# The opening weight loads and the last projection stores of a transformer block: blocks interleaved, 32 matmul passes made 16 transposes, a drain moved into the next stage

## The reference: what is computed

```python
mx = (silu(c) @ w_ada + b_ada)           # 6 x 1024 modulations; mz likewise from c_ctx
u  = x * (1 + mx[1]) + mx[0]             # modulated stream; context by mz
h  = u @ w_in                            # 1024 -> 1824 columns (context: 544 of them)
# A: latent attention, 6 heads (rank 256 for q, 128 for kv, shared rotary key)
# B: grouped attention, 6 query heads on 2 kv heads, RMS-normalised, 2-D rotary
# C: gated convolution of width 3
x  = layer_norm(ALPHA * x + mx[2] * (concat(A, B, C) @ w_o))
x  = layer_norm(ALPHA * x + mx[5] * (relu(x * (1 + mx[4]) + mx[3]) @ w1) ** 2 @ w2)
```

## Time and profile before

| | us |
|---|---|
| three runs: median (lowest to highest) | 3210.21 (3207.03 to 3212.64) |
| the profiled execution, its own time | 3208.03 |
| its span | 3206.2 |
| PE busy in the span | 3057.0 (95%) |
| DVE busy | 2299.8 (72%) |
| 16 DMA engines, queue q1 | 45.9% of their span |

### The profile page before, as it was taken

How to read it: one execution, slowest core, us unless ns; L and a number is a source line. 1 busy time by engine, 2 the same in 40 slices (tenths; PEclk the granted TensorE clock), 3 DMA queues, 4 the chain that set the end, 5 groups by cost and what they waited for, 6 DMA issues and landing times. The chain is left out here.

```text
span 3206.2 us, 38685 instructions
## 1 busy us (share of the span) xinstructions
PE 3057.0 (95%) x13729; PEld 2270.5 (71%) x13729; DVE 2299.8 (72%) x3190; ACT 1343.1 (42%) x1915; POOL 1368.1 (43%) x817
## 2 busy tenths in 40 slices
PE   4999968999999999999999997999999999999997
PEld 2888855565565656656566876888788888888786
DVE  3354446777777777777767788877777767788778
ACT  2232322434444444443443445555555543533441
POOL 0233301576776767755653225333333224323420
PEclk6999978999999999999999998999999999999999
DMA  6222378124332323221214678444733388887784
GB/s 238 61 78 86 97 228 287 56 61 103 89 76 68 73 62 89 61 66 37 49 40 163 241 279 311 159 157 157 290 145 148 141 316 291 302 310 292 271 307 144
DMA packets 235418, 515.49 MB, mean 161 GB/s; under 512 B 26673, under 2 KB 101809, under 8 KB 223025
## 3 DMA queue, kind: packets, MB, share of 16 engines
q1 hardware_dynamic: 227856, 484.97, 45.9%
q10 hardware_dynamic: 7392, 28.31, 2.4%
HBM read 352.44 MB, written 160.76 MB: 160 GB/s over the span
## 5 line engine op out<-in xcount | busy, mean ns | idle before, releaser
L1138 DVE TENSOR_REDUCE h_mpart<-a_mx 128x1 f32<-128x512 f32 x920 | 568.7, 636 | 266.1 <-PE a_mx L1238 257.4
L1075 POOL TENSOR_TENSOR a_acc_p<-a_acc_p,a_pf 128x1024 f32<-128x1024 f32 x240 | 581.0, 2421 | 213.4 <-ACT a_pf L1118 188.0
L1118 ACT ACTIVATE a_pf<-o_y 128x1024 f32<-128x1024 f32 x432 | 442.3, 1024 | 483.1 <-PE o_y L1264 482.6
L2273 PE MATMUL f_bank<-slots,f_wx 128*128 128x512 f32 x2304 | 573.4, 391 | 6.9 <-DMA slots<-s_uc 6.9
L2281 PE MATMUL f_bank<-slots 128*128 128x512 f32 x2128 | 505.4, 390 | 4.7 <-DVE slots L2052 2.5
L2273 PEld LDWEIGHTS f_bank<-slots,f_wx 128*128 128x128 f32 x2304 | 434.6, 189 | 99.1 <-DMA slots<-s_uc 8.5
L2281 PEld LDWEIGHTS f_bank<-slots 128*128 128x128 f32 x2128 | 399.4, 188 | 90.5 <-DVE slots L2052 4.2
L2219 POOL TENSOR_TENSOR f_work<-raw_rows 128x512 f32<-128x512 f32 x160 | 220.4, 1379 | 378.5 <-DVE f_wx L2045 366.6
L2228 POOL TENSOR_TENSOR f_y<-f_y,raw_rows 128x1024 f32<-128x1024 f32 x72 | 195.8, 2719 | 346.1 <-DMA raw_rows<-in_w 346.1
L2066 DVE TENSOR_TENSOR f_work<-f_work,f_bank 128x512 f32<-128x512 f32 x256 | 174.4, 681 | 133.7 <-ACT f_work L1944 122.5
L523 PE MATMUL p_main<-win_hi,u_hi 128*128 128x512 f32 (+2 forms) x528 | 198.2, 375 | 27.6 <-PEq L75 22.6
(11 more groups left out here) (277 smaller groups left out, 5354.7 us busy)
## 6 DMA issues: line engine op xcount, KB each, us to landing
raw_rows<-s_hx SPq DMA_DIRECT2D x112, 512.0 KB, 4.3
f_y<-in_w SPq DMA_DIRECT2D x104, 512.0 KB, 5.4
raw_rows<-in_w SPq DMA_DIRECT2D x72, 512.0 KB, 5.9
raw_rows<-in_w SPq DMA_DIRECT2D x32, 1024.0 KB, 4.8
s_hx<-stream SPq DMA_DIRECT2D x128, 256.0 KB, 2.7
s_hx<-f_work SPq DMA_DIRECT2D x96, 256.0 KB, 2.0
a_wa<-in_w_ada SPq DMA_DIRECT2D x8, 2048.0 KB, 9.3
slots<-s_uc ACTq DMA_DIRECT2D x10, 1024.0 KB, 15.2
```

The lines of the kernel that those rows point to most:

```text
L1075: nc.gpsimd.tensor_tensor(acc[:, :], left[:, :], pf[(b * KT + kt) % NPF][:, :], ALU.add).then_inc(added_p, 1)
L1118: nc.scalar.activation(pf[n % NPF][:, :], sc[n % 2][:, :], ACT.Exp, scale=SCALES[0 if is_mla(b) else 1]).then_inc(exped, 1)
L1138: nc.vector.reduce_max(mpart[b % 2][:, s, k:k + 1], mx[c % 2][:, 0:CHUNKS[k][1]], AX.X).then_inc(mx_read, 1)
L2273: mm = nc.tensor.matmul(by_pair(bank[:, m % 8, :]), w[:, k], x[s][:, :, k * P:(k + 1) * P], start=(k == 0 and j == 0), stop=(k == 3 and j ...
```

## The change

In the first stage SP issues `w_in` blocks 0, 1 and 2 each behind a `w_ada` block (2, 3 and 4), and blocks 3 to 7 behind the context tile. ACT and DVE split blocks 0 to 2 before their part in the modulations, and the rest behind it. The row is turned by 16 `transpose` instructions, each over 2 partitions at the start of a strip, into four PSUM banks, and the bias is added in four parts. The last projection tile's 13 stores no longer stand in the projection: SP issues the seven key/value ones and the two of the convolution at the start of the expansion, ACT the four of the queries behind its first three items. Their semaphore is waited for by SP ahead of `load_ckv` part 2 and by ACT ahead of `load_first_heads`.

```diff
@@ stage_modulate
-        SLOTS, ROWS = 3, 4
+        SLOTS, ROWS, BETWEEN = 3, 4, 3
-        ps = ctx.enter_context(nc.psum_tensor("ada_ps", [P, 512], F32))
+        ps = ctx.enter_context(nc.psum_tensor("ada_ps", [P, 4, 512], F32))
@@ SP
             for k in range(KD):
                 need(sp, w_used, k - SLOTS + 1)
                 sp.dma_start(w[:, k % SLOTS, :], a["w_ada"][k * P:(k + 1) * P, 0:NM]).then_inc(w_in[k % SLOTS], 16)
+                if 2 <= k < 2 + BETWEEN:
+                    w_in_rows(k - 2)
             tile(0)
-            for k in range(KD):
+            for k in range(BETWEEN, KD):
                 w_in_rows(k)
@@ ACT
-            act.wait_ge(w_used, KD)
-            nc.scalar.activation(row_sb[:, :], row_ps[:, :], ACT.Copy).then_inc(turn_step, 1)
             for k in range(KD):
+                if k == BETWEEN:
+                    act.wait_ge(w_used, KD)
+                    nc.scalar.activation(row_sb[:, :], row_ps[:, :], ACT.Copy).then_inc(turn_step, 1)
                 act.wait_ge(rows_in[k % ROWS], 16 * (k // ROWS + 1))
                 nc.scalar.activation(g.w_hi[:, k], rows[k % ROWS], ACT.Copy).then_inc(w_hi_set, 1)
-                if k == 0:
+                if k == BETWEEN:
                     act.wait_ge(g.modulated, 1)
@@ DVE
+            for k in range(BETWEEN):
+                low(k)
...
-            nc.vector.tensor_tensor(g.mods[:, 0:16, :], ps[:, 0:32].rearrange("p (m c) -> p m c", c=2),
-                                    g.b_ada[:, 0:16, None].to_broadcast([P, 16, 2]), ALU.add).then_inc(turn_step, 1)
+            for c in range(4):
+                m = slice(4 * c, 4 * c + 4)
+                ins = nc.vector.tensor_tensor(g.mods[:, m, :], ps[:, c, 0:8].rearrange("p (m c) -> p m c", c=2),
+                                              g.b_ada[:, m, None].to_broadcast([P, 4, 2]), ALU.add)
+            ins.then_inc(turn_step, 1)
...
-            for k in range(KD):
+            for k in range(BETWEEN, KD):
                 low(k)
-                if k == 0:
+                if k == BETWEEN:
                     dve.wait_ge(g.uhi_set, 1)
@@ PE
-                mm = nc.tensor.matmul(ps[:, 2 * m:2 * m + 2], row_sb[:, (m % 4) * P:(m % 4 + 1) * P], g.ident[:, 32 * c:32 * c + 2], start=True, stop=True)
+                strip = slice(32 * c, 32 * c + 2)
+                mm = nc.tensor.transpose(ps[:, c, 2 * (m % 4):2 * (m % 4) + 2], row_sb[strip, (m % 4) * P:(m % 4 + 1) * P], g.ident[strip, strip])
@@ stage_project
+        g.late_kv = lambda eng: store_kv(eng, CT + TT - 1, g.late_stored)
+        g.late_x = lambda eng: store_x(eng, CT + TT - 1, g.late_stored, conv=False)
+        g.late_conv = lambda eng: store_x(eng, CT + TT - 1, g.late_stored, heads=False)
@@ SP, end
-            store(CT + TT - 1, True)
-            sp.wait_ge(stored, stores_before(CT + TT))
+            sp.wait_ge(hi_out, CT + TT)
+            sp.wait_ge(lo_out, CT + TT)
+            sp.wait_ge(v_set, CT + TT)
+            sp.wait_ge(stored, stores_before(CT + TT - 1))
@@ ACT, end
-            act.wait_ge(hi_out, CT + TT)
             act.wait_ge(lo_out, CT + TT)
-            store_x(act, CT + TT - 1)
@@ stage_expand, SP
+            g.late_kv(sp)
+            g.late_conv(sp)
             load(1)
             store_set(1, 3, g.kn, slice(0, CTX))
+            sp.wait_ge(g.late_stored, 16 * LATE_STORES)
             load_ckv(sp, g, 2, slice(CTX + QB, KEYS))
@@ ACT
             for c in range(3):
                 item(c, 1, c, 0, CTX)
+            g.late_x(act)
...
                 if b == 0:
+                    act.wait_ge(g.late_stored, 16 * LATE_STORES)
                     load_first_heads(act, g, 0, first_heads_in)
```

More of the change, by code:

```diff
@@ L196, in modulate_tile @@
     return last
+LATE_STORES = 13
 def stage_project(nc, g, a):
@@ L243, in stage_project @@
         block = ctx.enter_context(nc.Block())
-        STORES_C, STORES_X = 7, 13
+        STORES_C, STORES_X = 7, LATE_STORES
         STEPS_C, STEPS_X = 9, 11
@@ L281, in schedule, with store_x, store_kv @@
             out(n, n, True)
-        def store_x(eng, n):
+        def store_x(eng, n, done=stored, heads=True, conv=True):
             raw = lambda t: t.bitcast(F32)
             q = bass.ds((n - CT) * P, P)
[L286 to L290, removed]
+            if heads:
+                for part, (ta, tb) in enumerate(((a_hi, b_hi), (a_lo, b_lo))):
+                    eng.dma_start(g.cq[part][:, :, q].rearrange("c p t -> p c t"), raw(ta[:, 1:3])).then_inc(done, 16)
+                    eng.dma_start(g.qg[part][:, q].rearrange("(c p) t -> p c t", p=P), raw(tb[:, 1:4])).then_inc(done, 16)
+            if conv:
+                eng.dma_start(g.conv_p[:, :, q].rearrange("c p t -> p c t"), c_st[:, 0:2]).then_inc(done, 16)
+                eng.dma_start(g.conv_b[:, :, q].rearrange("c p t -> p c t"), c_st[:, 2:4]).then_inc(done, 16)
+        def store_kv(eng, n, done=stored):
+            raw = lambda t: t.bitcast(F32)
+            tok = bass.ds(n * P, P)
+            for part, (ta, tb, tk) in enumerate(((a_hi, b_hi, k_hi), (a_lo, b_lo, k_lo))):
+                eng.dma_start(g.ckv[part][:, tok], raw(ta[:, 0])).then_inc(done, 16)
+                eng.dma_start(g.kg[part][:, tok], raw(tb[:, 0])).then_inc(done, 16)
+                eng.dma_start(g.kpe[part][:, tok], raw(tk[:, :])).then_inc(done, 16)
+            eng.dma_start(g.vg[:, :, bass.ds(n, 1)].rearrange("h p o c -> p h (o c)"), v_st[:, :].rearrange("p (h c) -> p h c", h=HKV)).then_inc(done, 16)
+        g.late_kv = lambda eng: store_kv(eng, CT + TT - 1, g.late_stored)
+        g.late_x = lambda eng: store_x(eng, CT + TT - 1, g.late_stored, conv=False)
+        g.late_conv = lambda eng: store_x(eng, CT + TT - 1, g.late_stored, heads=False)
         @block.sync
@@ L308, in store @@
                 sp.wait_ge(v_set, n + 1)
[L309 to L316, removed]
+                store_kv(sp, n)
+                if is_x:
                     store_x(sp, n)
@@ L563, in open_expansion @@
     sem = lambda n: g.expansion.enter_context(nc.semaphore("e_" + n))
+    g.late_stored = sem("late_stored")
     g.ckv_in = [sem(f"ckv_in{i}") for i in range(3)]
```

## The result

| | before | changed |
|---|---|---|
| median of 6 runs each, us | 3210.66 | 3189.45 |
| lowest run | 3207.03 | 3186.64 |
| the profiled execution's own time | 3208.03 | 3198.81 |
| its span | 3206.2 | 3196.8 |

The ratio is 0.9948, 95% interval 0.9935 to 0.9961, that is 12.5 to 20.9 us faster; the forecast was 6.4 us. One of the six runs of before took 9967.36 us, three times the others; the ratio is of the fast runs and leaves it out, and without it the median of before is 3210.21. On two other occasions the changed kernel came to 0.9951 (0.9938 to 0.9964) and 0.9966 (0.9952 to 0.9979). The three agree, at 14.4 us in the mean. Medians of the same kernel scatter by several us (3189.5, 3195.3, 3196.4), and the two medians of the table lie 21 us apart, just over the upper end of the interval.

A forecast was written before the change was run, and what follows sets the result against it. PE, 95% busy, had two gaps, ended by DVE's last subtraction and by 13 stores. 4.2 + 2.2 = 6.4 us gave 3201.6 from the profiled run or 3203.8 from the median; forecast 3203, range 3198 to 3208.5.

The forecast's parts named there:

- the second of its two parts: Boundary and expansion: late stores let the expansion start 6.0 us earlier, of which 2.2 us are kept; bounds 0 and 6.0.
- The first part: First stage: ends at 55.3 instead of 59.48, 4.2 us earlier; realistically 2.5 to 6.5.
- 16 x 0.214 = 3.4 us: First stage, turning the row: 16 transposes priced like the projection's, 3.4 us instead of 6.99, saving 3.6.
- Rival D: First stage: transposes in four strips run side by side, 0.9 us, 8.9 us gained in all, 3201; chance 0.08.
- I take 7.1 us: First stage: three `w_in` blocks, 2.80 MB at 392 GB/s, delay the end of the `w_ada` stream by 7.1 us; bounds 5 to 8.1.
- three more of 0.19 us: First stage: the bias addition becomes four, adding 0.6 us; bounds 0 and 1.
- The expansion starts 6.0 us earlier: Boundary: with no stores between last split and expansion, PE starts at 436.4 instead of 442.36.
- 3.8 turn into longer waits on `s_kn` and `s_qr`: Expansion: of the 6.0 us of compute, 3.8 go back to ACT's waits on these stores, leaving 2.2.
- at 480 the expansion is just at the pace of the DMA engines: Expansion: it can come no earlier than its DMA stream, which gains only 2.5 us of idle time.
- Rival A: Expansion: it keeps its full 6.0 us, 10.2 us gained in all, 3199; chance 0.18.
- rival C: First stage: the mixed stream falls to 280 GB/s, costing 15.3 instead of 7.1 us; kernel 1.8 us slower, 3212; chance 0.06.
- Rival B: Boundary and expansion: the second part gives nothing, 4.2 us alone remain, 3205; chance 0.16.

The follow-up runs named there:

- turn_full: The changed kernel with each of the 16 transposes over all 128 partitions instead of a strip's two; one execution, 0.23 us per transpose.
- turn_product: The changed kernel with the 16 transposes replaced by ordinary products over the same two-partition strips; one execution, turning took 4.15 us.
- part2: The changed kernel with the old first stage, so only the late stores are new; ratio to the kernel before 0.9992 (0.9982 to 1.0003).
- slots4: The turns kernel with four `w_ada` slots instead of three and three `w_in` buffers; one execution, last `w_ada` block 3.3 us earlier than in turns.
- turns: The kernel before with only the 16 transposes and four bias additions new, `w_in` blocks and stores as before; ratio 0.9977 (0.9966 to 0.9987).
- ckv_later: The changed kernel with SP loading ckv part 2 behind the first `s_qn` store instead of ahead; ratio to the kernel before 0.9978 (0.9967 to 0.9990).
- heads_later: The changed kernel with ACT issuing the first head's four loads later, after its b = 0 work; ratio to the kernel before 0.9966 (0.9952 to 0.9980).
- light_part1: part1 with two thirds of the first `s_qn` and `s_kn` stores, 2.1 MB, moved to the end of SP's program; expansion 97.0 us against 97.2.
- part1: The kernel before with only the first stage new, the projection's last stores left in place; ratio 0.9960 (0.9946 to 0.9974).

## Why the prediction was wrong

It put the time between 3198 and 3208.5; the median was 3189.45. It named the right places, and the size of the second of its two parts came out within the interval. The first part, forecast at 4.2 us, brought 11.25 in the profile. It was mis-sized in three terms, all the same way.

1. **"16 x 0.214 = 3.4 us"** (the turning). Measured 0.45 to 0.63 us, 2.8 to 3.0 less. The step took the price of a transpose over 128 partitions for one over two, the row of the same operation but not of the same height. turn_full gives 3.68 us for the full ones, so the reading was right and its transfer was wrong. The bound "nothing can save more than the 6.99 us" held it; the value within the bounds was chosen badly. Rival D had the right size (0.9 us), by strips side by side. The runs do not show whether strips overlap; turn_product, in the same strips, takes 4.15 us.

2. **"I take 7.1 us"** (three blocks in the stream). Measured 3.65 against the profile of before (1.5 against part2's, which has longer gaps). The step said that engines 0.94 to 1.02 busy leave no idle time to fill. The rows of before already held the contradiction: 346 GB/s at 0.94 busy beside 427 at 1.02. slots4 shows that the missing 80 GB/s were room: it ran at 422 GB/s where turns ran at 358, at nearly the same busy share. The lower bound of 5 us rested on another ground (what flows before 27.68 might yield) and was broken too.

3. **"three more of 0.19 us"** (bias addition). The four took 0.38 us together, 0.2 more than the one.

Together 2.9 + 3.45 + 0.4 = 6.8 us on top of 4.2, that is 11.0; the profile has 11.25. The rest of the first stage went as worked out: DVE's 13.4 us behind the modulations took 13.15 (35.08 to 48.23) without a stop, the early subtractions cost nothing, and block 7 of `w_in` came in time.

**The boundary.** "The expansion starts 6.0 us earlier": 6.1 in part2. "3.8 turn into longer waits on `s_kn` and `s_qr`": 4.6 to 5.6 were given back, but not there. The two waits it names became shorter (4.86 to 2.19 us, 0.90 to 0.34), and two that had not been there came in: 5.45 us on the store of the context's `s_kn`, and 8.02 us on the first `s_qn`. The first is the step that the prediction left out: the nine late stores stand ahead of that store. SP's timelines, before and after:

```profile
445.98 0.38 SPq L628 DMA_DIRECT2D s_kn<-e_st_hi  x1
```

```profile
431.92 0.60 SPq L650 DMA_DIRECT2D s_kn<-e_st_hi  x1
```

That is 3.6 and 7.3 us behind PE's first product. Its second half then landed 7.7 us after its issue instead of 5.9, at 440.3, which is where ACT's wait ends. The first `s_qn` store, issued 11 us behind PE's first product in both kernels, landed 16.9 and 20.7 us after its two issues where before it took 4.2 and 5.3. `load_ckv` 2 now goes out 2 us ahead of it instead of 7, and the first heads' loads come behind it; ckv_later and heads_later, which move these, each take this wait away and put another in its place.

The premise "at 480 the expansion is just at the pace of the DMA engines" is not borne out either: light_part1 has none of the waits on stores from which it was read, and its expansion is no shorter. So the size of this part was right by luck in part: a sum over the stream's idle time, where new waits did the taking back. The 2.2 us net were 1.5 in part2, and 1.7 between the first profile of the changed kernel and part1's (attention 2.1 earlier, 0.4 of it from the first stage). Rival A (the 6.0 us kept) and rival C (a mixed stream at 280 GB/s) are ruled out, A by the 4.6 to 5.6 us that the expansion gave back, C by 421 GB/s. Rival B, that this part gives nothing, is not: the profiles speak against it with 1.5 to 1.7 us, but the times of part2 allow it.

**Bandwidth.** The Trainium skill (DMA: Bandwidth & Descriptors, Specifications) gives about 358 GB/s for a core. The runs do not keep to it: 421 to 424 GB/s over 14 us in the changed kernel. The rates of before that lay near it, 346 and 357, went up with a fourth slot, and so were not a limit of the memory. The term would have been 7.8 us by that figure, further from the measured 3.65 than 7.1.

**Left open.** The ratios of the changed kernel say 14 us, its profiles have the attention 11.7 to 13.2 us earlier. The intervals cover this. Some of it may be the gaps of the old stream, which differ by 2 us between profiles; whether the runs of before without a profile have more of them is not known. Nor is it known whether an execution that is not profiled gives less back in the expansion. No version with a ratio is faster than the changed kernel beyond the interval.

## What to carry to other kernels

A busy share of the DMA engines near 1 does not mean that the stream is full: compare GB/s between stretches, and look at the spacing of the blocks on their reader; where single gaps stand out, ask for more at a time before calling it bandwidth. Price an operation by a row of its own shape: a transpose over two partitions had little in common with one over 128. Time taken from a barrier comes back where the next stage is near the pace of its transfers; here reordering them moved the wait, and only fewer bytes in that stretch shortened it. And a wait seen in a profile need not cost its length: light_part1 lost part1's 7.8 us of waits on stores and its expansion was 0.2 us shorter.

## What the hardware showed unexpectedly

- Over two partitions a float32 transpose took 0.028 us at a granted clock of 1.00 and 0.039 at 0.50; over 128 partitions 0.23 at 0.50; an ordinary product over two partitions 0.13 a pass at 0.55.
- The `w_ada` stream of 1 MB blocks ran at 346 GB/s from 2 to 24 us with three slots and 389 with four, both at a DMA busy share of 0.95 to 0.96; from 14 to 21 us at 358 and 422, at 0.98 and 1.01.
- A store of 768 KB that landed in 4.2 us before took 16.9 us in the changed kernel, with 1.5 MB of loads issued 2 us ahead of it and other loads and stores behind it.
- PE's granted clock while it turned the row was 1.00 in some profiles of the same program and 0.50 in others (turn 0.45 or 0.62 us); the projection began between 48.08 and 49.09.
